# The causal mask of stick-breaking attention moves from two vector operations to products on the tensor engine, and one pair of norm sums moves to an earlier place

## What is computed

```python
past = np.arange(kv_len)[None, :] < np.arange(q0, kv_len)[:, None]
z = jnp.einsum('bhtd,bhsd->bhts', qh[:, :, q0:kv_len], kh[:, :, :kv_len])
log_keep = jnp.where(past, jax.nn.log_sigmoid(-z), 0.0)
between = lax.cumsum(log_keep, axis=3, reverse=True) - log_keep
w = jnp.where(past, jnp.exp(jax.nn.log_sigmoid(z) + between), 0.0)
outs.append(jnp.einsum('bhts,bhsd->bhtd', w, vh[:, :, :kv_len]))
```

## Time and profile before

| | |
|---|---|
| runs | 1053.3, 1053.97, 1055.74 us; median 1053.97 us |
| the profiled execution's own time | 1056.51 us |
| its span, first to last instruction | 1054.7 us |
| PE | busy 1022.3 us, 97% of the span |
| DVE | busy 671.2 us, 64% |
| ACT | busy 510.9 us, 48% |
| POOL | busy 70.5 us, 7% |
| mean granted clock of TensorE | 0.993 |

### The profile page before, as it was taken

The page is one execution under the profiler, slowest core; times in us unless marked ns, Lnnn a source line. Parts: engine busy times, 40 slices in busy tenths (PEclk is TensorE's granted clock), DMA queues, the critical chain, the costliest instruction groups (busy, mean ns, idle before and its releaser), DMA issues.

```text
span 1054.7 us, 16426 instructions
## 1 busy us (share of the span) xinstructions
PE 1022.3 (97%) x7038; PEld 886.6 (84%) x7038; DVE 671.2 (64%) x761; ACT 510.9 (48%) x586; POOL 70.5 (7%) x84
## 2 busy tenths in 40 slices
PE   7999999999999999999999999999999999999997
PEld 5996888888989887978989897899658878888886
DVE  5566578676768676668777766354579765444444
ACT  6467464344346426554444444455467454443434
POOL 0000300000000000001011000000237000000000
PEclk9999999999999999999999999999989999999999
DMA  7642358666665662458688875223000344545541
GB/s 265 208 161 80 148 182 287 223 231 245 204 235 174 217 183 63 160 195 303 238 316 285 277 260 208 106 81 120 1 1 2 139 168 174 199 170 189 189 169 41
DMA packets 33469, 187.10 MB, mean 177 GB/s; under 512 B 3712, under 2 KB 7552, under 8 KB 14720
## 3 DMA queue, kind: packets, MB, share of 16 engines
q1 hardware_dynamic: 25344, 155.08, 42.5%
q0 software_dynamic: 7200, 27.27, 7.2%
q10 hardware_dynamic: 864, 3.88, 1.0%
HBM read 181.09 MB, written 1.05 MB: 173 GB/s over the span
## 4 chain that ended last, share of the span: by engine, by line
PE 88%; DVE 5%; ACT 4%; DMA 2%; issue 1%; DVEq 0%; SPq 0%; ACTq 0%
PE PS L277 12%; PE PS L278 12%; PE PS L279 12%; PE PS L602 11%; PE PS L603 11%; PE PS L604 11%; PE PS L1098 2%; DMA raw<-wstream 2%; PE PS L635 1%; PE PS L327 1%; PE PS L329 1%; PE PS L328 1%; DVE w_lo L264 1%; ACT w_hi L260 1%; PE PS L1332 1%
## 5 line engine op out<-in xcount | busy, mean ns | idle before, releaser
L264 DVE TENSOR_TENSOR w_lo<-raw,w_hi 128x2048 fp32r<-128x2048 f32 x139 | 318.4, 2292 | 200.1 <-ACT w_hi L260 199.7
L260 ACT ACTIVATE w_hi<-raw 128x2048 fp32r<-128x2048 f32 x141 | 269.2, 1911 | 176.9 <-PE PS L279 93.1
L602 PE MATMUL PS<-w_hi,a_hi 128*128 128x512 f32 x512 | 204.0, 398 | 2.4 <-DVE w_lo L264 2.4
L603 PE MATMUL PS<-w_lo,a_hi 128*128 128x512 f32 x512 | 200.6, 392 | 0.0
L604 PE MATMUL PS<-w_hi,a_lo 128*128 128x512 f32 x512 | 200.6, 392 | 0.0
L277 PE MATMUL PS<-a_hi,w_hi 128*128 128x256 f32 (+1 forms) x512 | 155.1, 303 | 0.4 <-DVE a_lo L462 0.4
L278 PE MATMUL PS<-a_lo,w_hi 128*128 128x256 f32 (+1 forms) x512 | 152.0, 297 | 0.0
L279 PE MATMUL PS<-a_hi,w_lo 128*128 128x256 f32 (+1 forms) x512 | 151.8, 297 | 0.0
L277 PE MATMUL PS<-h_hi,w_hi 128*128 128x256 f32 x528 | 149.8, 284 | 0.7 <-DVE h_lo L794 0.7
L279 PE MATMUL PS<-h_hi,w_lo 128*128 128x256 f32 x528 | 149.6, 283 | 0.0
L278 PE MATMUL PS<-h_lo,w_hi 128*128 128x256 f32 x528 | 149.6, 283 | 0.0
(11 more groups left out here) (345 smaller groups left out, 1248.9 us busy)
## 6 DMA issues: line engine op xcount, KB each, us to landing
raw<-wstream SPq DMA_DIRECT2D x142, 1024.0 KB, 4.8
modraw<-wmod POOLq DMA_DIRECT2D x48, 512.0 KB, 5.0
U<-CU SPq DMA_DIRECT2D x28, 142.0 KB, 2.8
cst<-cst ACTq DMA_DIRECT2D x1, 1632.0 KB, 9.3
mlw<-mlw ACTq DMA_DIRECT2D x1, 1280.0 KB, 5.5
X<-xT SPq DMA_DIRECT2D x2, 512.0 KB, 5.2
CROW<-crow POOLq DMA_DIRECT2D x1, 1024.0 KB, 5.2
CTX<-ctxT POOLq DMA_DIRECT2D x1, 1024.0 KB, 8.5
```

What stands on the lines that cost most here:

```text
L260: nc.scalar.activation(w_hi[:, slot, :], raw[:, rslot, :], ACT.Copy).then_inc(S("hi_done"), 1)
L264: dve.tensor_tensor(w_lo[:, slot, :], raw[:, rslot, :], w_hi[:, slot, :].bitcast(F32), ALU.subtract).then_inc(S("lo_done"), 1)
L602: nc.tensor.matmul(out, a_hi[:, k, src, ts], wh, start=k == 0, stop=False, skip_group_check=True)
L603: nc.tensor.matmul(out, a_hi[:, k, src, ts], wl, start=False, stop=False, skip_group_check=True)
```

## The change

The mask becomes a bias on the scores: a 128 x 128 block that holds 0 where the key lies ahead of the query and -1e30 elsewhere is added to each diagonal block by a product of an identity with it, both in bfloat16, in the same accumulation as the scores. With a score of -1e30, the log term of the position and its weight both come out as zero, so DVE's two mask operations per pair go (L1961 and L1976), and PE waits for the operation ahead of each instead. DVE makes the two bfloat16 operands once, by two copies of 128 x 128. Apart from this, in the second and third feed-forward blocks' code (`if f`) `norm_tokens_pe` is issued between unit u0 and unit u0 + 1 where a block has these sums; only the second block has both `f` and `norm`, so it is the only one that moves.

```diff
             if norm:
                 gate_up(u0, u0 % SLOTS, 0, 4, None, True)
-                gate_up(u0 + 1, (u0 + 1) % SLOTS, 1, 4, None, True, lambda: norm_tokens_pe(pe, norm))
+                if f:
+                    norm_tokens_pe(pe, norm)
+                gate_up(u0 + 1, (u0 + 1) % SLOTS, 1, 4, None, True, None if f else lambda: norm_tokens_pe(pe, norm))
...
                 if g == 0:
                     pe.wait_ge(S("qkn_done"), 3)
                     pe.wait_ge(S("og_rs"), 1)
+                    pe.wait_ge(S("sb_bias"), 2)
...
-                    nc.tensor.matmul(PS[:, b, 0:256], kT[:, 0:P], qT, start=True, stop=True)
-                    i = nc.tensor.matmul(PS[:, b, 256:384], kT[:, P:T], qT[:, P:T], start=True, stop=True)
+                    nc.tensor.matmul(PS[:, b, 0:256], kT[:, 0:P], qT, start=True, stop=False, skip_group_check=True)
+                    nc.tensor.matmul(PS[:, b, 0:128], SBIDENT, SBBIAS, start=False, stop=True, skip_group_check=True)
+                    nc.tensor.matmul(PS[:, b, 256:384], kT[:, P:T], qT[:, P:T], start=True, stop=False,
+                                     skip_group_check=True)
+                    i = nc.tensor.matmul(PS[:, b, 256:384], SBIDENT, SBBIAS, start=False, stop=True,
+                                         skip_group_check=True)
...
             def sb_between(g):
-                pe.wait_ge(S("sb_keep"), g + 1)
+                pe.wait_ge(S("sb_v"), 2 * g + 1)
...
             def sb_out(g):
-                pe.wait_ge(S("sb_w"), g + 1)
+                pe.wait_ge(S("sb_exp"), g + 1)
...
             qk_norm(0)
             lo(dve, 13)
+            dve.wait_ge(S("csb_loaded"), 16)
+            dve.wait_ge(S("cst_loaded"), 16)
+            dve.tensor_copy(SBBIAS, csb[:, 128:256]).then_inc(S("sb_bias"), 1)
+            dve.tensor_copy(SBIDENT, ident).then_inc(S("sb_bias"), 1)
...
                 dve.scalar_tensor_tensor(m, z, 0.0, l, ALU.max, ALU.add).then_inc(S("sb_v"), 1)
-                dve.wait_ge(S("sb_v"), 2 * g + 1)
-                diagonal = m.rearrange("p e (b n) -> p e b n", b=3)[:, :, 0:3:2, :]
-                dve.tensor_tensor(diagonal, diagonal, md, ALU.mult).then_inc(S("sb_keep"), 1)
...
-            def sb_mask(g):
-
-                w = SBZ[:, g % 3].rearrange("p e (b n) -> p e b n", b=3)[:, :, 0:3:2, :]
-                dve.wait_ge(S("sb_exp"), g + 1)
-                dve.tensor_tensor(w, w, md, ALU.mult).then_inc(S("sb_w"), 1)
...
-    csb = np.concatenate([after, before, ones, before], 1)
+    csb = np.concatenate([after, (before - 1.0) * np.float32(1e30)], 1)
```

More of the change, by code:

```diff
@@ L62 @@
 N_CST = 416
-CSB = {"tri": (0, 128), "sbmask": (128, 384)}
-N_CSB = 512
+CSB = {"tri": (0, 128), "sbbias": (128, 128)}
+N_CSB = 256
 CS2 = {}
@@ L140, in program @@
         csb = at("csb", 188, N_CSB)[:, :]
-        tri, sbmask = csb[:, 0:128], csb[:, 128:512]
+        tri = csb[:, 0:128]
         WGL = at("WGL", 152, 128)[:, :]
@@ L159, in program @@
         SBL = at("SBL", 114, 2 * 768)[:, :].rearrange("p (g e n) -> p g e n", g=2, e=2)
-        SBK = at("SBK", 121, 768)[:, :].rearrange("p (e n) -> p e n", e=2)
+        SBBIAS = at("SBBIAS", 122, 128, BF16)[:, :]
+        SBIDENT = at("SBIDENT", 123, 128, BF16)[:, :]
         SBM = at("SBM", 125, 2 * 768)[:, :].rearrange("p (g e n) -> p g e n", g=2, e=2)
@@ L1946, in _ @@
             i.then_inc(S("gla_out"), 1)
-            dve.wait_ge(S("csb_loaded"), 16)
-            md = sbmask.rearrange("p (b n) -> p b n", b=3)[:, 0:3:2, :].unsqueeze(1).to_broadcast([P, 2, 2, P])
             def sb_keep(g):
@@ L1983, in _ @@
             sb_add(1)
-            sb_mask(0)
             sb_keep(3)
             sb_add(2)
-            sb_mask(1)
-            sb_mask(2)
             sb_add(3)
-            sb_mask(3)
             dve.wait_ge(S("act_lo"), ACT_LO["o1"] + 2)
```

## The result

The changed kernel takes 1058.23 us in the median of 20 runs (1052.86 to 1061.06), the kernel before 1054.74 in the median of 20 runs (1052.62 to 1056.59): a ratio of 1.0026, with a 95% interval of 1.0017 to 1.0036. That is slower, by some 2.8 us (0.0026 x 1054.7; the two medians lie 3.5 us apart), clear of the noise though only a quarter of a percent. The forecast was 1053.4 within 1049.8 to 1057.0. The profiled execution after took 1058.48 us, 2.0 more than the one before.

A forecast was written before the change was run, and what follows sets the result against it. PE was taken to bound the kernel, with 88% of the chain that ended last. The mask's +3.8 us and the moved sums' -4.35 us gave -0.55, taken as -0.6 on the median: 1053.4 us, range 1049.8 to 1057.

The forecast's parts named there:

- part two: Second feed-forward block: earlier norm sums remove PE's 2.44 us wait and the half clock behind it, -4.35 us in all.
- Rival D: Second feed-forward block: the hole stays because the copy to `w_hi` meets something else late; at most 1057.8 us, chance 0.08.
- the mechanism of the steps: Stick-breaking scores: switches between 64-row and full products cost about 0.20 us each and end head overlap; pair 0.8 to 2.9 us.
- B: Stick-breaking scores: steps are cheap, a pair takes about 1.9 us or less; sum -3.6, 1050.3 us; chance 0.34.
- C: Stick-breaking scores: a step costs 0.30 us or more, a pair 3.6; sum +2.3, 1056.3 us; chance 0.14.
- the removed masks buy nothing beside the longer scores: Stick-breaking stage: DVE's holes are hidden behind PE's longer scores, so the removed masks buy nothing up to pair 3's scores.
- The copies for the bias: Ahead of the first scores: two 128 x 128 copies costed at nothing, at most 1.7 us late start for both.
- the walk at full clock: Stick-breaking stage followed operation by operation: PE starts at 92.82, pairs 0 and 1 end at 98.6, stage at 124.8.
- +3.8: Stick-breaking stage with the mask on PE: stage ends at 124.8 instead of 120.86, bounds +0.7 to +6.7 us.
- a granted clock under 1.00: Sign of being wrong, between 92.8 and 125 us; the half clock behind one hole had cost 1.6 us.
- The range: Whole kernel: median between 1049.8 and 1057 us, leaving out about 2 in 10.

The follow-up runs named there:

- experiment 2: Kernel before with only the norm sums of the second feed-forward block moved ahead, masks left on DVE: 1051.05 us, ratio 0.9962.
- 10: Changed kernel with both heads' scores first, one accumulation start per bank, and the norm sums back in their old place: 1052.48 us, ratio 0.9979.
- 5: Changed kernel with both heads' scores first, the four bias products behind them, and one accumulation start per bank: 1049.08 us, ratio 0.9938.
- 7: As 5, but one bias product of 256 columns per head instead of two of 128: 1048.67 us, ratio 0.9936.
- 9: As 5, but six zero products instead of ten ahead of the sums of pair 0: 1048.51 us, ratio 0.9935.
- 8: Changed kernel with each head's two score products and then its two bias products, head by head: 1051.64 us, ratio 0.9968.
- experiment 4: Changed kernel without the bias products, so no causal mask at all: 1049.92 us, ratio 0.9941.
- 6: Changed kernel with a zero product of 512 columns behind each of its 16 bias products: 1057.06 us, ratio 1.0016.
- 1: Kernel before with the mask change alone, the second block's norm sums left in their old place: 1061.07 us, ratio 1.0055.
- 11: The changed kernel measured again without alteration, 12 runs: 1057.02 us, ratio 1.0015 to the kernel before.
- 3: Changed kernel with both heads' scores first, then four bias products, each score product still starting its own accumulation: 1049.76 us, ratio 0.9937.

## Why the prediction was wrong

**Right: part two.** Forecast -4.35 us; -4.0 by experiment 2 alone, 4.3 by 10 against 5, and the landmarks of seven profiles agree with 4.35, those of three (2, 7 and 9) don't. The sums went ahead, the wait went, the fills were followed by L603 with no idle time, and from the fills to L636 it took 466.46 - 460.1 = 6.4 us (three of the four fills start at 460.34; the first lies some 0.2 before), as in the first block. Rival D is out.

**Right: the mechanism of the steps.** A pair of scores was to go from 0.8 to 2.9 us and went to 2.73. Two sizes in that term were off and nearly cancel, which is luck: the way into a bias product costs 0.20 us (93.53 - 92.90 = 0.63, less the 0.43 of the score product's two passes), the way out 0.10 (93.69 - 93.53 = 0.16, less the 0.06 of its columns), where the forecast had 0.15 and 0.20. Four of each, with 1.28 and 0.23 for the columns, make 2.71. That an uninterrupted pair uses both halves of the array, and that the bias products end this, is shown by 5 and 8 beside the change: the same products take 1.19 us with both heads side by side, 2.13 head by head and 2.73 interleaved. The rule of the Trainium skill that the prediction weighed (TensorEngine Tiling (Array Packing), Tiling Modes) holds here. Rivals B and C are out: with 2.73 a pair is neither under 2.5 nor at 3.6. That the removed masks buy nothing beside the longer scores has no run of its own; experiment 4 gives only their worth with short scores, 2.2 us. The copies for the bias took 0.22 us each at 89.24, well before the scores, and cost nothing.

**Wrong: the walk at full clock.** The step that failed is "PE starts at 92.82 as now. Pairs 0 and 1 end at 98.6", and with it every later time of the walk up to "the stage ends at 124.8". All of them were taken at 2.4 GHz. Up to 96.3 the trace follows the walk; then the clock is at half, pair 1 ends at 99.6 instead of 98.6, L954 with the 0.22 us behind it takes 101.84 - 99.60 = 2.24 us where 0.96 was walked, and pair 3 and the sums behind it are slowed in the same way. What it costs can be estimated from 8 and 6, whose pairs are shorter and longer and which both hold the clock: 2.13 us a pair ends at 122.07 and 3.59 at 126.27, 2.88 us per us of a pair. At 2.73 that is 123.8, if the end moves evenly in between; if each of the four pairs counts in full from 6 downward, it is 122.8. So the steps cost an estimated +2.0 to +2.9 where the forecast had +3.8, and the clock cost 5.4 to 6.4 us, where the forecast had nothing. That agrees with some 14 us at half clock in this profile, which can lose 7 at the most. With +2.9 the sum would have been about -1.4 us, near the three runs at high clock (1052.9 to 1054.5). The prediction named a granted clock under 1.00 here as a thing that would make it wrong, with the 1.6 us of one fall beside it, but gave it no chance and no term in the sum. It took a fall to need a hole in PE's work, as in the earlier trace rows, and this stretch had none. The earlier trace rows could have warned it: the 0.94 there is a fall within this very stage, at 105 to 108 us.

**The rival that decides is thus one I didn't list:** the new order of products itself lowers the clock. Its condition by the runs: four bias products in a pair each with a change of kind on both sides (the change, 1 and 11) lowered it in all three profiles, the same four in two groups (8) or one (3, 5, 9, 10) in none, and the same eight changes of kind with a long product in each group (6) in none. What the chip measures is not settled by this. PE is on record as busy without a break ahead of each of these falls, and in 6 as well, so the busy share isn't what tells them apart. The Trainium skill, TensorE: Matmul & The Clock Gate, has a section A second HAM failure mode: psum-queue depth-cycling, on a clock that goes back and forth because of very short idle moments between groups of matmuls. That is near to what is seen here, with the drains as such moments, though no idle time is on record; its cause there, the cycling through banks, was not tried here. Nor did I try why some executions keep the clock. So that the order lowers the clock is shown, and why it does stays open.

**The range** ended at 1057.0 because it took its upper bound from dearer steps. The 1.2 us by which the median lies above it are less than the clock's share, and with the steps alone the time would have been inside.

## What to carry to other kernels

Before a full-array product is put between products on half of the rows, count the changes of kind and see whether two of the small products ran side by side: both heads' scores first and the bias products behind them cost 0.4 us a pair (1.19 against 0.8), the interleaved order 1.9. The mask operations taken from DVE gave at most 2.2 us of the 7.0 us that DVE was relieved of, so such a move pays only if PE gets the work nearly free; in the good order both edits together gave 6.5 to 6.9 us (versions 5, 7 and 9), most of it from sums that stand where their inputs are ready. And in a walk through a timeline, ask of each new stretch of short, drained products what clock it will be granted, with a price for the answer, even where PE never stands still.

## What the runs showed of the chip that I had not expected

The granted clock fell from 2.4 to 1.2 GHz, for about 7 us each time, while PE was on record as busy but for 0.22 us, and 16 added zero products kept it at 2.4 GHz and made the stage 3.0 us shorter. The same hole of 2.44 us was followed by half clock in two profiles (before and 1) and by full clock in one (10). And a fall in an untouched stretch, between 760 and 780 us, comes in some executions and not in others: between the two landmarks the profiles have 91.1 us (before, 1, 5, 6) or 90.3 (3, 4, 7) with it and 87.8 or 88.7 without (2, 8, 9, 10, 11 and after), so that single spans of two kernels can differ by 3 us for a reason that has nothing to do with the change.
